# A two-block transformer kernel: the spatial block's feed-forward with seven products per tile pair

## The reference, cut to what matters

```python
D_FF_2 = 2816
CONV_F_WIDTH = 3

def _conv_ffn(x, w_up, conv_f_w, conv_f_b, w_down):
    h = _causal_depthwise_conv(x @ w_up, conv_f_w, conv_f_b)
    gate, val = h[..., :D_FF_2], h[..., D_FF_2:]
    return (jax.nn.silu(gate) * val) @ w_down

x = _layernorm(DEEPNORM_ALPHA * x + mix, ln1_g, ln1_b)
ffn = _conv_ffn(x, w_up, conv_f_w, conv_f_b, w_down)
x = _layernorm(DEEPNORM_ALPHA * x + ffn, ln2_g, ln2_b)
```

## Time and profile before

| | |
|---|---|
| Time, three executions | 3771.41, 3779.22 and 3779.77 us, median 3779.22 |
| Span of the profiled execution | 3767.9 us |
| Time of that execution beside its span | the page gives none; the median is 11.3 us above the span |
| Busy share of the span | TensorE 96%, VectorE 57%, GpSimd 48%, ScalarE 34% |

### The profile page before, as it was taken

One profiled execution on the slowest core, in us unless ns is written; L12 is line 12 of the kernel. 1 busy time (PEld: TensorE's weight loads), 2 busy tenths in 40 slices (PEclk: granted clock), 3 DMA queues, 4 the chain that ended last, 5 costly groups with the idle time before them and its releaser, 6 DMA issues.

```text
span 3767.9 us, 51125 instructions
## 1 busy us (share of the span) xinstructions
PE 3631.0 (96%) x17973; PEld 2944.0 (78%) x17973; DVE 2148.5 (57%) x3586; ACT 1263.4 (34%) x2051; POOL 1812.5 (48%) x1926
## 2 busy tenths in 40 slices
PE   6999999999999899999989999999998999999997
PEld 5778878888887677777767888887787778888886
DVE  6863454333344466665565566668599464444455
ACT  5432241111113655555544233332315332222223
POOL 2543276555551522222217677778463285344342
PEclk9999999999999999999999999999999999999999
DMA  7321013232320011111111111111111111111121
GB/s 234 124 69 40 29 39 112 89 95 95 95 84 24 24 45 40 46 40 46 40 34 51 45 58 47 49 54 48 35 61 45 34 45 56 45 49 51 40 72 45
DMA packets 244572, 223.53 MB, mean 59 GB/s; under 512 B 12586, under 2 KB 194488, under 8 KB 244425
## 3 DMA queue, kind: packets, MB, share of 16 engines
q1 hardware_dynamic: 218368, 170.04, 14.8%
q10 hardware_dynamic: 26057, 51.52, 4.3%
HBM read 217.27 MB, written 4.26 MB: 59 GB/s over the span
## 4 chain that ended last, share of the span: by engine, by line
PE 59%; DVE 4%; ACT 2%; POOL 1%; issue 1%; DVEq 0%; ACTq 0%; POOLq 0%
PE PS L749 6%; PE PS L750 6%; PE PS L751 6%; PE PS L1219 3%; PE PS L1220 3%; PE PS L1221 3%; PE PS L776 3%; PE PS L778 3%; PE PS L777 3%; PE PS L871 2%; PE PS L869 2%; PE PS L870 2%; PE PS L883 2%; PE PS L885 2%; PE PS L884 2%; PE PS L1265 2%
## 5 line engine op out<-in xcount | busy, mean ns | idle before, releaser
L749 PE MATMUL PS<-UH,WH 128*128 128x512 f32 x1808 | 716.8, 396 | 22.4 <-ACT UU L2213 8.0
L3748 POOL TENSOR_SCALAR WH<-RAW 128x1024 fp32r<-128x1024 f32 x203 | 226.0, 1113 | 1033.0 <-issue 386.4
L3751 POOL TENSOR_TENSOR WL<-RAW,WH 128x256 fp32r<-128x256 f32 x809 | 704.1, 900 | 16.9
L751 PE MATMUL PS<-UH,WL 128*128 128x512 f32 x1808 | 708.1, 392 | 0.0
L750 PE MATMUL PS<-UL,WH 128*128 128x512 f32 x1808 | 707.9, 392 | 0.0
L749 PEld LDWEIGHTS PS<-UH,WH 128*128 128x128 f32 x1808 | 340.8, 188 | 103.1 <-issue 15.7
L751 PEld LDWEIGHTS PS<-UH,WL 128*128 128x128 f32 x1808 | 340.3, 188 | 73.8
L750 PEld LDWEIGHTS PS<-UL,WH 128*128 128x128 f32 x1808 | 341.0, 189 | 70.2 <-issue 0.2
L2423 DVE TENSOR_TENSOR X<-PS,X 128x512 f32<-128x512 f32 x320 | 215.3, 686 | 222.7 <-PE PS L935 213.5
L3376 DVE SCALAR_TENSOR_TENSOR FY<-FZ,PV,FY 128x512 f32<-128x512 f32 x88 | 82.9, 942 | 329.8 <-ACT FY L2343 328.9
L933 PE MATMUL PS<-WH,HH 128*128 128x512 f32 x640 | 253.9, 397 | 10.3 <-POOL WL L3751 5.6
(11 more groups left out here) (418 smaller groups left out, 8136.0 us busy)
## 6 DMA issues: line engine op xcount, KB each, us to landing
RAW<-in_mlp_w_dram SPq DMA_DIRECT2D x104, 512.0 KB, 4.2
ADM<-in_ada_w_dram ACTq DMA_DIRECT2D x96, 256.0 KB, 3.2
RAW<-in_w_up_dram SPq DMA_DIRECT2D x44, 512.0 KB, 3.9
ADR<-in_ada_w_dram ACTq DMA_DIRECT2D x32, 512.0 KB, 3.8
WR<-in_od_w_in_dram SPq DMA_DIRECT2D x32, 512.0 KB, 4.2
W2R<-in_mlp_w_dram SPq DMA_DIRECT2D x24, 512.0 KB, 3.3
RAW<-in_w_down_dram SPq DMA_DIRECT2D x22, 512.0 KB, 3.2
RAW<-in_ev_w_in_dram SPq DMA_DIRECT2D x20, 512.0 KB, 3.8
```

The source lines that it names most:

```text
L749: pe.matmul(bank(b)[0:width], wh, xh, start=(k == 0), stop=False)
L751: mm = pe.matmul(bank(b)[0:width], wl, xh, start=False, stop=(k == NK - 1))
L3748: pool.tensor_scalar(WH[slot][:, 0:n], r[:, 0:n], 1.0, 1.0, ALU.mult, ALU.mult).then_inc(S("w_hi"), 1)
L3751: ins = pool.tensor_tensor(WL[slot][:, c], r[:, c], WH[slot][:, c].bitcast(F32), ALU.subtract)
```

## The change

Group 0, two gate and two value tiles, stays as it was on TensorE: eight items of 24 matmuls. The other twenty pairs of a gate and a value tile take a round each. A round sees the weights as a matrix of two by two blocks (512 inputs by gate or value) and the input as one of two by two blocks (512 inputs by 512 tokens). It forms the four output blocks from seven products, p1 to p7, of four blocks of 128 inputs each: 12 matmuls with their three passes. The weight side needs four differences per round, t1 to t4, on VectorE (t3 with them). The input side needs four sums, s1 to s4, once, made by VectorE and GpSimd behind the first `up` items.

The order of a round is p1, p2, p6, p5, p7, p3, p4 (`round_`). p1 goes to bank r % 2 and is copied out before p6 and p7 are added onto it. The copy of what the bank then holds and the adding of the other products give the two halves of the gate and the value in GZ. ScalarE makes the high parts of the weights (`w_hi`), GpSimd the low parts (`w_lo`). The convolution's accumulators are PSUM banks 2 to 5, where ScalarE puts the last tap with the bias (`tap_2`). The gated rows go to a DRAM tensor. When all rounds are done, the down projection runs as a phase of eleven steps, with tiles of gated rows read back (`f_hi`, `f_lo`). Its 96 matmuls per step stay, in `down`. `t_rows` is gone here; rows of ln1 are loaded by DMA in four quarters, and VectorE scales X in sixteen steps of 1024 elements, two in each of rounds 2 to 9 (`residual`). The loops over groups are written out. The diff, cut to its core:

```diff
+FF_PLAIN = 2
+FF_ROUNDS = D_FF2 // P - FF_PLAIN
+FF_DOWN = D_FF2 // P // 2
...
+FF_ORDER = ("p1", "p2", "p6", "p5", "p7", "p3", "p4")
+FF_RES = 16
...
+tiles = [(tile_m(w, lambda it, m=m: m * P), 4 + m, m) for m in range(2)]
+tiles += [(tile_m(w, lambda it, m=m: m * P + D_FF2), 6 + m, 2 + m) for m in range(2)]
+plan.add("ffn", 1, tiles, 8)
...
+    def product(r, name, b, start):
+        pe.wait_ge(*past("fp_lo", 7 * r + FF_NTH[name]))
+        xh, xl, k0, c = moving[name]
+        wh, wl = FPH[name], FPL[name]
+        for k in range(4):
+            if r == 0 and name in made:
+                pe.wait_ge(*past(made[name], k + 1))
+            w = slice(k * P, (k + 1) * P)
+            pe.matmul(bank(b), wh[:, w], xh[:, k0 + k, c], start=start and k == 0, stop=False, skip_group_check=True)
+            pe.matmul(bank(b), wh[:, w], xl[:, k0 + k, c], start=False, stop=False, skip_group_check=True)
+            mm = pe.matmul(bank(b), wl[:, w], xh[:, k0 + k, c], start=False, stop=(k == 3), skip_group_check=True)
+        mm.then_inc(S("fp_mm"), 1)
+    def round_(r):
+        b = r % 2
+        if r >= 2:
+            pe.wait_ge(*past("fp_c", 4 * (r - 1)))
+        product(r, "p1", b, True)
+        if r:
+            pe.wait_ge(*past("fp_d", 3 * (r - 1) + 1))
+        product(r, "p2", 6, True)
+        pe.wait_ge(*past("fp_c", 4 * r + 1))
+        product(r, "p6", b, False)
+        if r:
+            pe.wait_ge(*past("fp_d", 3 * r))
+        product(r, "p5", 7, True)
+        pe.wait_ge(*past("fp_c", 4 * r + 2))
+        product(r, "p7", b, False)
+        pe.wait_ge(*past("fp_c", 4 * r + 3))
+        product(r, "p3", 7, False)
+        pe.wait_ge(*past("fp_d", 3 * r + 2))
+        product(r, "p4", b, False)
...
-    t_rows(5, 0, 1)
...
-    t_rows(5, 2, 3)
...
+    for r in range(FF_ROUNDS):
+        round_(r)
+    for j in range(FF_DOWN):
+        last = j == FF_DOWN - 1
+        for h in range(2):
+            down(j, h, (BY_BLOCK if last else BY_COLUMN)[h])
...
+    def w_hi(r, name):
+        if r == 0:
+            act.wait_ge(S("gemm_done"), item0 + 5 + FF_SLOT[name][0])
+        else:
+            act.wait_ge(*past("fp_mm", 7 * (r - 1) + FF_NTH[name]))
+        sem, count = {"p1": ("f_ra", 16 * (r + 1)), "p2": ("f_ra", 16 * (r + 1)), "p3": ("f_rb", 16 * (r + 1)),
+                      "p6": ("ft2", r + 1), "p5": ("ft1", r + 1), "p7": ("ft3", r + 1), "p4": ("ft4", r + 1)}[name]
+        act.wait_ge(*past(sem, count))
+        act.activation(FPH[name][:, :], src[name], ACT.Copy).then_inc(S("fp_hi"), 1)
+    def copy(r, nth, out, b):
+        act.wait_ge(*past("fp_mm", 7 * r + nth))
+        act.activation(out, bank(b), ACT.Copy).then_inc(S("fp_c"), 1)
+    def tap_2(r, m, z, b):
+        c = r + FF_PLAIN + 22 * m
+        act.activation(bank(b), z, ACT.Identity, bias=taps("conv_f_b_2", c), scale=taps("conv_f_w_2", c, 2))\
+            .then_inc(S("fp_y"), 1)
+    z = [GZ[:, m, 2 + h * HALF:2 + (h + 1) * HALF] for m in range(2) for h in range(2)]
+    def last_gate(r):
+        copy(r, 7, z[1], r % 2)
+        act.wait_ge(*past("fp_c", 4 * r + 4))
+        if r:
+            act.wait_ge(*past("fp_s", 2 * r))
+        tap_2(r, 0, z[1], 3)
+    def silu(r, h):
+        act.wait_ge(*past("fp_cv", 4 * r + (4 if h else 1)))
+        act.wait_ge(*past(f"f_sent{h}", 16 * (2 + r)))
+        act.activation(FO[h][:, :], bank(2 + h), ACT.Silu).then_inc(S("fp_s"), 1)
...
+    for k in range(4):
+        s_hi(3, k)
+    first_item(1, 0)
+    w_hi(0, "p1")
+    w_hi(0, "p2")
+    for k in range(4):
+        s_hi(2, k)
+    first_item(1, 1)
+    w_hi(0, "p6")
+    first_item(1, 2)
+    first_silu(1, 0)
+    first_item(1, 3)
+    w_hi(0, "p5")
+    for k in range(4):
+        s_hi(4, k)
+    first_silu(1, 1)
+    for k in range(4):
+        s_hi(1, k)
+    w_hi(0, "p7")
+    w_hi(0, "p3")
+    for r in range(FF_ROUNDS):
+        w_hi(r, "p4")
+        if r:
+            last_gate(r - 1)
+            act.wait_ge(*past("fp_cv", 4 * r))
+        else:
+            act.wait_ge(*past("f0_conv", 8))
+        copy(r, 1, z[0], r % 2)
+        if r:
+            silu(r - 1, 1)
+        nxt = r + 1 < FF_ROUNDS
+        if nxt:
+            w_hi(r + 1, "p1")
+        act.wait_ge(*past("fp_d", 3 * r + 1))
+        if r == 0:
+            act.wait_ge(*past("f0_f", 4))
+        else:
+            act.wait_ge(*past("fp_s", 2 * r - 1))
+        tap_2(r, 0, z[0], 2)
+        if nxt:
+            w_hi(r + 1, "p2")
+        silu(r, 0)
+        copy(r, 3, z[2], r % 2)
+        if nxt:
+            w_hi(r + 1, "p6")
+        copy(r, 4, z[3], 7)
+        if nxt:
+            w_hi(r + 1, "p5")
+            w_hi(r + 1, "p7")
+            w_hi(r + 1, "p3")
+        act.wait_ge(*past("fp_d", 3 * r + 3))
+        if r:
+            act.wait_ge(*past("fp_f", 2 * r))
+        tap_2(r, 1, z[2], 4)
+        tap_2(r, 1, z[3], 5)
+    f_hi(0)
+    last_gate(_R)
+    silu(_R, 1)
+    for j in range(1, FF_DOWN):
+        f_hi(j)
...
+    def t4(r):
+        if r == 0:
+            dve.wait_ge(S("gemm_done"), PH["ffn"]["I"] + 8)
+        else:
+            dve.wait_ge(*past("fp_mm", 7 * (r - 1) + 7))
+        dve.wait_ge(*past("ft2", r + 1))
+        dve.tensor_tensor(FPR["p4"][:, :], b21, FT2[:, :], ALU.subtract).then_inc(S("ft4"), 1)
+    def sum_(r, nth, m, h, b, c):
+        dve.wait_ge(*past("fp_mm", 7 * r + nth))
+        dve.wait_ge(*past("fp_c", 4 * r + c))
+        x = GZ[:, m, 2 + h * HALF:2 + (h + 1) * HALF]
+        dve.tensor_tensor(x, bank(b), x, ALU.add).then_inc(S("fp_d"), 1)
+    def conv(r, m, h, y_nth, cv_nth):
+        dve.wait_ge(*past("fp_y", 4 * r + y_nth))
+        c = r + FF_PLAIN + 22 * m
+        y = bank(2 + 2 * m + h)
+        x = lambda back: GZ[:, m, 2 + h * HALF - back:2 + (h + 1) * HALF - back]
+        fch.done(dve.scalar_tensor_tensor(out=y, in0=x(1), scalar=taps(c, 1), in1=y, op0=ALU.mult, op1=ALU.add))
+        dve.scalar_tensor_tensor(out=y, in0=x(2), scalar=taps(c, 0), in1=y, op0=ALU.mult, op1=ALU.add)\
+            .then_inc(S("fp_cv"), 1)
+    def gated(r, h):
+        dve.wait_ge(*past("fp_s", 2 * r + h + 1))
+        dve.wait_ge(*past("fp_cv", 4 * r + (3 if h else 2)))
+        dve.tensor_tensor(FO[h][:, :], bank(4 + h), FO[h][:, :], ALU.mult).then_inc(S("fp_f"), 1)
...
+    for r in range(FF_ROUNDS):
+        if r:
+            t4(r)
+            conv(r - 1, 0, 1, 4, 4)
+        sum_(r, 2, 0, 0, 6, 1)
+        if r:
+            gated(r - 1, 1)
+        conv(r, 0, 0, 1, 1)
+        if r + 1 < FF_ROUNDS:
+            t1_t2(r + 1)
+        if 2 <= r < 2 + FF_RES // 2:
+            residual(2 * r - 4)
+            residual(2 * r - 3)
+        sum_(r, 5, 1, 1, r % 2, 3)
+        if r + 1 < FF_ROUNDS:
+            t3(r + 1)
+        sum_(r, 6, 1, 0, 7, 2)
+        if r == _R:
+            f_lo(0, 0, 0)
+            f_lo(0, 0, 1)
+        conv(r, 1, 0, 2, 2)
+        conv(r, 1, 1, 3, 3)
+        gated(r, 0)
+    f_lo(0, 1, 0)
+    f_lo(0, 1, 1)
+    conv(_R, 0, 1, 4, 4)
+    gated(_R, 1)
+    dve.wait_ge(*past("x5", FF_RES))
...
+    for r in range(1, FF_ROUNDS):
+        if r + 1 < FF_ROUNDS:
+            raw_b(r + 1)
+            raw_a(r + 1)
+        send(0, r + 1, 0, "fp_f", 2 * r - 1)
+        send(1, r + 1, 1, "fp_f", 2 * r)
+        if r in (4, 6, 8):
+            residual_rows(r // 2 - 1)
...
+    w_lo("p1")
+    w_lo("p2")
+    for k in range(4):
+        s2_lo(k)
+    w_lo("p6")
+    w_lo("p5")
+    w_lo("p7")
+    w_lo("p3")
+    for r in range(FF_ROUNDS):
+        w_lo("p4")
+        if r + 1 < FF_ROUNDS:
+            for name in ("p1", "p2", "p6", "p5"):
+                w_lo(name)
+            w_lo("p7")
+            w_lo("p3")
+    for j in range(FF_DOWN):
+        for t in range(2):
+            down_tile(j, t)
```

More of the change, by code:

```diff
@@ L227, in transposition_order @@
     out += norm(1) + norm(2) + gate(2) + gate(3) + norm(3) + norm(4)
[L228 removed]
+    out += [("w", 0), ("s", 0)] + [(s, h, i) for h in range(2) for s in "cd" for i in range(4)]
+    out += [("u", 5, h, k) for h in range(2) for k in range(NK)]
     return out
@@ L406, in S, with past @@
             return sems[name]
+        def past(name, count):
+            return S(name), (PAST[name][1] if name in PAST else 0) + count
         prow = param_rows(A)
@@ new lines, in down @@
+                def down(j, h, order):
+                    s = j % 2
+                    for i, (tb, mh) in enumerate(order):
+                        n = 16 * j + 8 * h + i
+                        if n < 8:
+                            name, count = FD_ENTRY[n]
+                            pe.wait_ge(*past(name, count))
+                        else:
+                            pe.wait_ge(*past("fd_add", n - 7))
+                        o = bank(FD_BANK[n % 8])
+                        x = slice(tb * P, (tb + 1) * P)
+                        wh, wl = WDH[s][mh], WDL[s][mh]
+                        pe.wait_ge(*past("fd_w", 2 * j + 2 if h or order != BY_COLUMN[0] else 2 * j + mh + 1))
```

(65 more changed lines are left out.)

415 lines of the change are left out of this document (294 added, 121 removed), and 4 rows, old and new, of the table PAST.

## The result

| | before | after |
|---|---|---|
| Median of 20 executions each | 3773.36 us | 3778.10 us |
| Profiled execution: span | 3767.9 us | 3773.0 us |
| TensorE busy, matmuls | 3631.0 us, 17973 | 3590.0 us, 17701 |

A forecast was written before the change was run, and what follows sets the result against it. It took TensorE's matmuls, busy 96% of the span, as the bound. Products -54.4, stall and clock in nineteen rounds +80.6, entry -5.8 and +6.4, exit +4.5 gave +31 us: 3810 us, forecast range 3795 to 3832, wide range 3765 to 3843.

The forecast's parts named there:

- stall at p6, 19 rounds: Each round, TensorE waits before p6 for ScalarE's copy of p1: 2.6 us beyond the cover of 8.16 us.
- The products: Twenty rounds of 84 instead of 96 matmuls on TensorE save 240 matmuls, 54.4 us, if TensorE never waits.
- The chain of 10.8 us: Steps from p3's last matmul through VectorE and ScalarE to the copy of p1: 10.8 us, bounds 10.4 to 11.6.
- The clock in every round: After each gap before p6 the granted clock falls, slowing p6's matmuls: 1.6 us per round, bounds 0 and 1.6.
- The rule on micro-idles: Skill rule that micro-idles between matmul groups make TensorE's clock swing; without it the sum is 30 us less.
- t4's price: The weight difference t4 on VectorE takes 0.68 us, as GpSimd idles then; by the contention rule alone 0.83.
- Rival 3: Residual, t1 and t2 collide with GpSimd, delaying p7's and p3's sums in eight rounds: +32 us, 3842 us; chance 0.10.
- Entry: Start of the rounds: -5.8 us from transposes and convolutions, +6.4 us for round 0's stall and one clock drop.
- Exit: End of the rounds: last value sum, roundings and subtractions delay the down phase, +4.5 us with a drop; bounds 0 and 9.
- The base: The median of the runs stands 11.3 us above the profiled span; the same was added to the forecast span.
- Rival 1: The stall before p6 is there but the clock stays: -3 us, 3776 us; chance 0.13.
- Rival 2: The chain hides under p4, p1 and p2: -55 us, 3724 us, or 3744 with 1 us per round; chance 0.17.

The follow-up runs named there:

- early_tile: The changed kernel with the gate tile of round 1 fetched ahead of its value tile; 3774.45 us, ratio 1.0005 to before.
- t4_twice: The changed kernel with t4 computed twice on VectorE, one after the other, from round 1 on; 3800.90 us, ratio 1.0078 to before.
- t4_gpsimd: The changed kernel with t4 of rounds 1 to 19 made on GpSimd instead of VectorE; 3740.28 us, ratio 0.9929 to before.
- own_t4: The changed kernel with t4 in its own buffer, made a round ahead, its rounding behind p1's copy, round 1's gate tile fetched early; 3716.87 us, ratio 0.9854 to before.

## Why the prediction was wrong, point by point

The place, the cause and the regularity of the wait were right; the sum was +31 us and the span grew by 5.1. From before to after, by the two traces:

| term | predicted | measured |
|---|---|---|
| 240 matmuls | -54.4 | -54.4 |
| stall at p6, 19 rounds | +50.2 | +39.3 (19 x 2.07) |
| clock in these rounds | +30.4 (19) | +11.6 (7 x 1.65) |
| entry: end of the eighth item | -5.8 | -8.5 |
| entry: p1 and p6 of round 0 | +6.4 | +1.5 and +5.0 |
| p7 of round 0, with clock | 0 | +7.9 (5.95 and 1.9) |
| exit | +4.5 | +1.1 |
| tail | 0 | -1.5 |
| rest | 0 | +3.1 |

(My 4.24 per round was 2.64 of stall and 1.6 of clock. The last line closes the sum to the 5.1 us between the spans. Some 2 us of it are the first matmul behind each gap, which stands 0.34 us ahead of the next where others stand 0.23; the remainder is not assigned.)

- **The products** (-54.4): right, and the down phase costs next to nothing more: it is full, at a clock of 1.00 (239.8 us from its first matmul to its last).
- **The chain of 10.8 us**: the step that failed first, in size. Every link is there, in the order given. It has 10.2 us. ScalarE's seed releases VectorE 0.81 us after its start, where I took 0.92; dependent multiply-adds start 0.80 apart, where I took 0.89; copy to seed is 0.62, where I took 0.70. I had taken single hand-overs of another stage and added the largest ones up, then gave 10.4 as the lower bound. The true value is outside my bounds.
- **The clock in every round**: the term that decided. I charged 1.6 us nineteen times, because in the trace of before the clock had fallen at ten gaps out of ten of 2.4 us or more. With the chain 0.6 us shorter the gap is 2.30, and there the same trace had said "three times in five". It fell in 7 of 19, and in early_tile in 9 of 19. So an error of 0.6 us in the chain carried most of one of 19 us in the clock. Even for 3.02 us "ten of ten" was too much: t4_twice has 15 of 19. These two terms were 30 us too high together, the whole sum 26; entry and exit took 2 us more than I had given them, tail and rest 1.6.
- **The rule on micro-idles** ("TensorE: Matmul & The Clock Gate", section "A second HAM failure mode: psum-queue depth-cycling" of the Trainium skill): this trace agrees in kind, for the clock swings with regular gaps. The section says nothing of a gap's length, and here the count goes with it: no fall in 19 rounds at 1.70 us, 7 at 2.30, 15 at 3.02.
- **t4's price**: I took 0.68; the group of the nineteen has 682 ns in the mean:

```profile
L3669 DVE TENSOR_TENSOR FPR_p<-RAW,FT 128x512 f32<-128x512 f32 x19 | 13.0, 682 | 0.0
L3649 DVE TENSOR_TENSOR FT<-RAW,RAW 128x512 f32<-128x512 f32 x18 | 17.0, 947 | 0.0
L3651 DVE TENSOR_TENSOR FT<-RAW,FT 128x512 f32<-128x512 f32 x18 | 16.7, 926 | 0.6
```

  t1 and t2 in the two rows under it, made while GpSimd works, take 0.94 us. So the layout decided, as argued: the rule of contention (the Trainium skill, "GPSIMD Engine Reference", section "Key points") bears on t1 and t2, and t4, beside which GpSimd idles (4.33 us before its next piece, at 3363.47), keeps its 0.68.
- **Rival 3** (residual, collisions): false. Gaps of rounds 2 to 9 are those of the later ones, 2.28 to 2.30. (Where the chain is shorter the early rounds do stand out a little: all gaps of t4_gpsimd over 0.76 us are in rounds 3 to 10.)
- **Entry**: two signs. The eighth item ended 2.7 us sooner than I had worked out; p1 of round 0 waited 1.5 us for its bank, and p6 3.4 of stall, where I had 4.8. And I costed tile 1 at nothing ("issued by SP at the start of a round and used 5 us later"), which is true of the steady rounds only: in round 0 SP stood in front of raw_b's wait, and ScalarE's queue carried that to p7, 7.9 us.
- **Exit**: one gap of 1.34 us at 3512.75, +1.1 us instead of +4.5 with a drop. VectorE's subtraction ends it (the idle time of 0.96 us is put down to line 3713). The piece that I worked out was right, 4 us behind p3 against 2.7 of p4; the two further banks that I added to it, and the drop, did not come.
- **The base**: I put 11.3 us around the span, from three executions. Twenty executions of before give 3773.36, 5.5 above it, and the profiled execution of after took 3774.77, 1.8 above its own span. 6 of the 32 us between forecast and time are this, 26 the sum.
- **Rival 1** (3776, the clock stays) came nearest to the time, but not for its reason: with the stall at 2.07 and seven falls the clock did not stay. **Rival 2**, the hidden chain at 3724, is not what this kernel does; own_t4, which takes t4 out of the chain, comes to 3717.

## To carry to other kernels

When an engine's queue stands on the path, an instruction put in it costs its start distance plus that of the engine it hands to; ask of each link who else could do it, and earlier, also at half the speed. Where a stall may or may not bring the clock down (here between 1.70 us, with no fall in 19, and 3.02, with 15), give the forecast as two cases, for half a microsecond moves it from one towards the other. A wait for a transfer in an in-order queue counts against every instruction behind it: after removing one wait, look where the late one goes, and look at the first round by itself.
